# A hybrid SSD and DeltaNet block on one core: constants ahead of the weights, and 64 bytes of fill

## What is computed

```python
h = rms_norm(x, g_mix_pre)
proj = h @ w_in            # z, xbc, dt, qkv, gate, b, a, m_gate
y_ssm = mamba2_branch(...)  # convolution, chunked SSD over the tokens, norm
y_gdn = gdn_branch(...)     # convolution, chunked gated DeltaNet, norm
mixed = gate_ssm * (y_ssm @ w_br_ssm) + gate_gdn * (y_gdn @ w_br_gdn)
x = x + rms_norm(mixed @ w_out, g_mix_post)
h = rms_norm(x, g_ffn_pre)
act = gelu(causal_dwconv(h @ w_ffn_gate, conv_ffn_w) + conv_ffn_b)
f = (act * (h @ w_ffn_up)) @ w_ffn_down
x = x + rms_norm(f, g_ffn_post)
e = sigmoid(x @ w_ple_gate) * (p @ w_ple_proj)
out = x + rms_norm(e, g_ple_post)
```

## Time and profile before

| | us |
|---|---|
| median of 3 runs | 2723.59 |
| lowest and highest run | 2722.64, 2727.72 |
| the profiled execution | 2735.69 |
| its span, first to last instruction | 2734.0 |

### The profile page before, as it was taken

The page is one execution under the profiler, slowest core; times in us unless marked ns, Lnnn a source line. Parts: engine busy times, 40 slices in busy tenths (PEclk is TensorE's granted clock), DMA queues, the critical chain, the costliest instruction groups (busy, mean ns, idle before and its releaser), DMA issues. The chain is left out here.

```text
span 2734.0 us, 29517 instructions
## 1 busy us (share of the span) xinstructions
PE 2588.0 (95%) x12016; PEld 2120.3 (78%) x12016; DVE 1484.3 (54%) x1175; ACT 536.3 (20%) x549; POOL 1065.3 (39%) x549
## 2 busy tenths in 40 slices
PE   6999999799989998989998799999999999999995
PEld 5888888577778887768876588888888888888774
DVE  4779776236665667541517744444444444444745
ACT  4100101456312323230023200000000000000431
POOL 2334333455544645423355433333333333333361
PEclk8999999999999999989999899999999999999997
DMA  5322222699756676453233211111111111112231
GB/s 198 108 92 85 100 94 87 193 288 273 227 179 181 172 199 176 134 169 138 92 139 102 83 47 47 46 53 55 46 46 46 46 46 46 46 49 74 78 108 62
DMA packets 276942, 304.06 MB, mean 111 GB/s; under 512 B 43821, under 2 KB 241786, under 8 KB 272762
## 3 DMA queue, kind: packets, MB, share of 16 engines
q1 hardware_dynamic: 246122, 248.88, 29.8%
q10 hardware_dynamic: 30736, 54.01, 5.4%
HBM read 216.35 MB, written 86.51 MB: 111 GB/s over the span
## 5 line engine op out<-in xcount | busy, mean ns | idle before, releaser
L436 PE MATMUL ps<-act_hi,w_hi 128*128 128x512 f32 x2288 | 913.0, 399 | 24.3 <-ACT ring_b L890 12.9
L440 PE MATMUL ps<-act_hi,w_lo 128*128 128x512 f32 x2288 | 902.8, 395 | 0.0
L439 PE MATMUL ps<-act_lo,w_hi 128*128 128x512 f32 x2288 | 898.9, 393 | 0.0
L421 POOL TENSOR_SCALAR w_hi<-w_raw 128x1024 fp32r<-128x1024 f32 x219 | 245.8, 1122 | 1443.5 <-PE ps L436 607.7
L423 POOL TENSOR_TENSOR w_lo<-w_raw,w_hi 128x1024 fp32r<-128x1024 f32 x219 | 579.7, 2647 | 18.3
L436 PEld LDWEIGHTS ps<-act_hi,w_hi 128*128 128x128 f32 x2288 | 432.8, 189 | 123.4 <-ACT ring_b L890 15.1
L439 PEld LDWEIGHTS ps<-act_lo,w_hi 128*128 128x128 f32 x2288 | 432.6, 189 | 97.2 <-issue 3.6
L440 PEld LDWEIGHTS ps<-act_hi,w_lo 128*128 128x128 f32 x2288 | 432.4, 189 | 92.5
L2034 DVE TENSOR_TENSOR tile<-ps,tile 128x1024 f32<-128x1024 f32 x112 | 135.7, 1221 | 107.9 <-PE ps L1584 106.5
L2472 DVE SCALAR_TENSOR_TENSOR ring_a<-xin,par,ring_a 128x1024 f32<-128x1024 f32 x108 | 185.1, 1714 | 11.8 <-DVE ring_a L2466 0.3
L1584 PE MATMUL ps<-f_hi,w_lo 128*128 128x512 f32 x480 | 189.3, 394 | 0.0
(11 more groups left out here) (288 smaller groups left out, 2942.9 us busy)
## 6 DMA issues: line engine op xcount, KB each, us to landing
w_raw<-in_w_in_dram SPq DMA_DIRECT2D x34, 1024.0 KB, 5.5
spill<-ring_b ACTq DMA_DIRECT2D x67, 512.0 KB, 2.7
w_raw<-in_w_ffn_gate_dram SPq DMA_DIRECT2D x17, 1024.0 KB, 5.4
w_raw<-in_w_ffn_up_dram SPq DMA_DIRECT2D x17, 1024.0 KB, 5.5
w_raw<-in_w_ffn_down_dram SPq DMA_DIRECT2D x16, 1024.0 KB, 4.8
qkv_a<-spill SPq DMA_DIRECT2D x8, 1536.0 KB, 8.2
dec_a<-cum_rows SPq DMA_DIRECT2D x16, 512.0 KB, 14.3
gdn_in<-hrow SPq DMA_DIRECT2D x8, 1024.0 KB, 9.9
```

Of the source, the lines that this page charges most:

```text
L421: nc.gpsimd.tensor_scalar(hi, raw, 1.0, 0.0, ALU.mult, ALU.add).then_inc(split_done, 1)
L436: first = nc.tensor.matmul(o, wh, mov[0][:, k, c], start=(k == 0), stop=False)
L439: nc.tensor.matmul(o, wh, mov[1][:, k, c], start=False, stop=False)
L440: last = nc.tensor.matmul(o, wl, mov[0][:, k, c], start=False, stop=(k == KD - 1))
```

## The change

The three tensors for weights are allocated behind the five small constants and a new tensor `fill` of 16 floats, 64 bytes, on each partition. `fill` is neither written nor read. No instruction changes.

```diff
-    w_raw = sb("w_raw", [P, 2, 2048])
-    w_hi = sb("w_hi", [P, 2, 1024], f32r)
-    w_lo = sb("w_lo", [P, 2, 1024], f32r)
     ident = sb("ident", [P, P])
     ones = sb("ones", [P, P])
     eps_t = sb("eps_t", [P, 1])
     par = sb("par", [P, 4, P])
     d_ch = sb("d_ch", [P, KD])
+    fill = sb("fill", [P, 16])
+    w_raw = sb("w_raw", [P, 2, 2048])
+    w_hi = sb("w_hi", [P, 2, 1024], f32r)
+    w_lo = sb("w_lo", [P, 2, 1024], f32r)
```

## The result

The changed kernel takes 2707.22 us (median of 4 runs, 2701.96 to 2708.47), the kernel before 2723.86 us in the same comparison (2722.64 to 2727.72). The ratio is 0.9931, with a 95% interval from 0.9913 to 0.9949: 16.6 us or 0.7% faster. A second set of runs of the same changed kernel, further down, gives 2703.73 against 2724.3 us, 20.6 us, ratio 0.9913 (0.9886 to 0.994). Two executions among those further down, one of 4201.87 us (w0_a64) and one of 6665.7 us (w192_a192), were in a slower state and stand in no median or ratio here. The forecast was 2723.6 us and no difference. The time lies in the range of 2704 to 2740 us, but the likeliest case was the wrong one.

What follows compares the result with a forecast made beforehand. TensorE, busy 2588.0 of 2734.0 us, was taken as the bound, mostly float32r matmuls 228.8 ns apart. 2735.7 + 0 + 0 + 0 = 2735.7 us profiled, 2723.6 us on the runs' scale; range 2704 to 2740 us.

Steps and rivals of the forecast that it cites:

- the likeliest case: Whole kernel: no difference from the kernel before, 2723.6 us on the runs' scale; chance 0.61.
- VectorE, ScalarE and GpSimd at 0: Vector, activation and gpsimd work: operands keep their remainder modulo 64 and none paces the long stage, so 0 us.
- The DMA term of -3.0 to +4.1 us: Weight loads might gain up to 3.0 us, qkv_a loads lose up to 4.1 us; opposite signs, so taken as 0.
- the 0 for TensorE's reads: Float32r matmuls at 228.8 ns each: the 14.3 ns excess was held not to come from addresses, so 0 us.
- the third reading: Float32r matmul durations of 388, 392 and 394 ns rotate among lines by stage; a cost tied to remainders would stay put.
- The first two readings: Evidence for 0 on TensorE: plain float32 and 128-column products showed no effect of how their operands were aligned.
- The second: Products of 128 columns last 275 ns with both operands at 0 past 256 and with both at 224.
- The first: Plain float32 product with its moving operand 224 past a multiple of 256 shows no excess, 214.5 ns a pass.
- The fourth reading: Within one unit of weights, loops step by 512, 2048 and 4096 bytes, so larger operand distances already occur, at one pitch.
- The collision rival: Float32r matmuls: weight and activation reads at equal remainders modulo 512 collide more, 25 us slower, 2748.6 us; chance 0.12.
- The rival by blocks of 256: Float32r moving operand touches 8 blocks instead of 9: 1.6 ns a matmul, 14.7 us faster, 2708.9 us; blocks together 0.15.
- The full gain (-132 us): Float32r matmuls: the whole 14.3 ns excess is misalignment and goes, giving 2591 us; chance 0.05.

Runs made afterwards that it cites:

- w0_a64: The changed kernel with 64 more bytes between w_lo and act_hi, against the changed kernel; 2727.2 us, ratio to before 0.999.
- w192_a192: The changed kernel without its 64-byte fill, new order kept; 2709.6 us, ratio to before 0.992.
- before_gap192: The kernel before, in its own order, with 192 unused bytes added behind d_ch; 2706.81 us, ratio to before 0.9928.
- w128_a0: The kernel before, in its own order, with 64 bytes of fill added behind d_ch; 2755.09 us, ratio to before 1.010.
- d192: The changed kernel without its fill and with a gap of 48 floats behind w_lo; 2758.36 us, ratio to before 1.012.
- d32: The changed kernel without its fill and with a gap of 8 floats behind w_lo; 2754.16 us, ratio to before 1.012.

## Why the prediction was wrong

**What held.** The bound was read rightly: nearly all of the gain is in the distance from one float32r matmul to the next, at 9.3 us for a nanosecond, and nothing else moved with the addresses. VectorE, ScalarE and GpSimd at 0 held. (The nine lines counted leave out 288 of the 9552 float32r matmuls of the trace, 3%, which changes nothing here.) The DMA term of -3.0 to +4.1 us is not to be seen: the weight loads land in 5.3 and 5.5 us in two profiles of the same kernel. The Trainium skill's rule in "DMA: Bandwidth & Descriptors", How a descriptor splits into AXI transactions, is neither contradicted nor shown by any run here.

**The step that failed** is the 0 for TensorE's reads: it was 2.2 ns on each float32r matmul, 228.89 to 226.67 ns, where anything over 0.6 ns was to count as wrong. In it, the third reading failed. I took the three durations, 388, 392 and 394 ns, which change lines from stage to stage, as proof that the cost doesn't hang on the operands' remainders: "a cost tied to the operands' remainders would stay with its line". The rotation was itself the sign of the cost. In the kernel before, three matmuls in a row take 6.67 ns more than three at 226.67 ns, and it isn't one of them that takes it: the mean distances from 1600 to 2500 us are 225.8 ns behind L436, 229.2 ns behind L439 and 231.7 ns behind L440. In another stretch the same three values stand behind other lines. Why they change places is not shown. With equal remainders the three values are one. I had the total of the excess, and a pattern in it that no size of operand explains, and set it aside because it didn't fit the one form of cost that I had in mind.

**The first two readings** were right as rows and proved nothing here. The second compared dd with nt, both at 0, and s_gdn with qk, both at 224, so the distance was 0 in both: the quantity that matters didn't vary. The first had a distance of 224 (s_ssm and xbc), but the plain float32 products tried don't show the effect. L1098 (512 columns of hrow with the weights ones; L1099 in the changed kernel) has a distance of 128 before and 192 after, and its median time from start to start is 429 ns in both kernels, as that of L799. So they were the wrong stand-in for float32r. The nearest row was near in shape and not in kind. That such a product takes two passes of the columns is a reading of this number (429 ns is twice 512 columns at 2.4 GHz, 213.3 ns); no run shows the passes themselves.

**The fourth reading** holds: larger distances, in steps of 512, don't count, and by before_gap192 256 doesn't either. It left just the remainder modulo 256 open, which the change alters, and I should have said that this was the one thing the trace couldn't exclude.

**The rivals.** The collision rival named the right quantity, the distance between weights and activations, with the wrong sign. I took equal remainders for the bad case. They are the good one, and the unequal ones carry the price: w128_a0, d192 and d32 take 30 to 34 us more than the kernel before beside them, where the rival had 25 us. The rival by blocks of 256 came out at 2708.9 us, 1.7 us from the measured time, but that nearness is luck: its pitch, 227.2 ns, is 0.5 ns off, and w192_a192, which touches as many blocks as before, gains as much. The full gain (-132 us) is out: 226.67 ns is still 12.2 ns over the 214.5 ns of a plain float32 pass.

**The Trainium skill**, "SBUF — State Buffer", Specifications (TRN2), gives lines of 16 bytes. What the prediction worked out from it, that moves by multiples of 64 bytes do nothing to any engine, did not hold: a distance of 32 bytes between the starts of two operands that are both aligned to 32 costs 233.3 against 226.7 ns. The line size itself is neither shown nor contradicted by that.

**The chances.** 0.61 on no difference was too much for a term of 9.3 us a nanosecond with no row for an aligned float32r operand. A chance that rests on stand-ins should have stayed nearer to even.

## What to carry to other kernels

Where float32r matmuls with a weight load each run back to back at the full clock, let the weights' buffers and the moving operands' buffers begin at the same remainder modulo 256. One unused tensor between them does it. Here that is worth 0.7%, while the layouts with the longest pitch cost up to 1.2%. Any edit that adds or removes a small tensor between the two can switch this on or off, so compare the start-to-start distance of the long stage before you credit an edit with a per cent. A regular pattern of a few nanoseconds in the durations of identical instructions is worth a test before it is set aside: here it was a cost with a cause.

## What the runs showed of the hardware that was not expected

- The distance between float32r matmuls of 512 columns, with a weight load each, took few values at the full clock: 226.7, 228.9, 231.1 and 233.3 ns in the steady stretches. These four lie 2.2 ns apart, a third of 6.67 ns, which is 16 columns at 2.4 GHz. Two more, 232.4 ns (distance 128) and 232.0 ns (act_lo alone displaced), don't fit that ladder.
- Distances of 32, 128 and 192 bytes between the operands' starts all cost 232.4 to 233.3 ns, 64 costs 228.9 or 233.3, and 0 and 256 modulo 512 cost 226.7 ns. Two paces are possible with the same addresses (distances 64 and 128). In w0_a64 the long stretch kept its slower pace over 4390 matmuls without a pause.
- At the lower clock level there was no excess in the kernel before: 0.427 us for 512 columns.
- The plain float32 matmuls read here show none of it: 429 ns for 512 columns at distances of 128, 192 and 224.

What stays open is the mechanism below this: why 226.67 and not 213 ns for 512 columns at 2.4 GHz, which reader waits for which, and why 64 can be cheaper than 32 or 192. Neither of the two kernels that displaced one operand alone matches one of the theories exactly.
